# Delta stage: gate rows and inverse norms spread by row-repeating transfers through DRAM

## The reference, cut to what matters

```
g      = -exp(a_log) * softplus(a + dt_bias)          one number per head and token
G      = cumsum(g) within a chunk                      [16 heads, 256 tokens]
decay  = exp(G[i] - G[j]) for i >= j, else 0           128 x 128 for each head and chunk
A      = -beta * (k k^T) * decay;  T = (I - A)^-1      solved by blocks
o      = (q k^T * decay) v_new + (q * exp(G)) state    v_new and state from T, k, v
out    = (o * 1/sqrt(mean(o^2) + eps) * norm_w * silu(z)) @ w_out
```

## Time and profile before

| | us |
|---|---|
| median of 3 runs | 2250.34 |
| lowest, highest | 2249.08, 2255.46 |
| the profiled execution | 2247.1 |
| its span in the trace | 2245.3 |
| Delta stage in the trace, about | 1691 to 2044 |

### The profile page before, as it was taken

The page is one execution under the profiler, slowest core; times in us unless marked ns, Lnnn a source line. Parts: engine busy times, 40 slices in busy tenths (PEclk is TensorE's granted clock), DMA queues, the critical chain, the costliest instruction groups (busy, mean ns, idle before and its releaser), DMA issues.

```text
span 2245.3 us, 41478 instructions
## 1 busy us (share of the span) xinstructions
PE 2114.8 (94%) x15546; PEld 1969.2 (88%) x15546; DVE 1447.5 (64%) x2478; ACT 1114.0 (50%) x1802; POOL 48.6 (2%) x63
## 2 busy tenths in 40 slices
PE   7998999999998999999999999999997898999998
PEld 7977889999978889989998989989987787978997
DVE  4457677775457677776657666666667877457565
ACT  4454455555443455554445454454446566546443
POOL 1002000000002000000000000000000000000000
PEclk9899999999899999999999999999998998999999
DMA  8422355553222445546554555555554433335552
GB/s 248 150 95 85 121 193 185 195 194 132 89 99 83 146 160 196 194 143 214 181 193 164 174 179 186 179 172 187 183 169 122 127 109 114 112 123 183 187 186 95
DMA packets 118577, 350.80 MB, mean 156 GB/s; under 512 B 23505, under 2 KB 36121, under 8 KB 117953
## 3 DMA queue, kind: packets, MB, share of 16 engines
q1 hardware_dynamic: 115248, 336.27, 45.1%
q0 software_dynamic: 3216, 12.97, 2.1%
HBM read 341.85 MB, written 7.34 MB: 156 GB/s over the span
## 4 chain that ended last, share of the span: by engine, by line
PE 73%; DVE 13%; ACT 6%; issue 4%; DMA 2%; POOL 0%; DVEq 0%; ACTq 0%; SPq 0%; POOLq 0%
PE bank L2074 22%; PE bank L2076 21%; PE bank L2075 21%; DVE wlo L1392 5%; ACT whi L934 3%; PE bank L2500 1%; DMA raw<-panels 1%; PE bank L2223 1%; DVE arena L1582 1%; PE bank L2100 1%; DVE arena L1431 1%; PE bank L2283 1%; DVE x L1442 1%; DMA relay<-arena 0%; DMA arena<-relay 0%
## 5 line engine op out<-in xcount | busy, mean ns | idle before, releaser
L2074 PE MATMUL bank<-xhi,whi 128*128 128x256 f32 x3496 | 1007.2, 288 | 14.4 <-DVE xlo L1778 5.4
L2075 PE MATMUL bank<-xlo,whi 128*128 128x256 f32 x3496 | 993.7, 284 | 0.0
L2076 PE MATMUL bank<-xhi,wlo 128*128 128x256 f32 x3496 | 993.1, 284 | 0.0
L1392 DVE TENSOR_TENSOR wlo<-raw,whi 128x1024 fp32r<-128x1024 f32 x623 | 740.1, 1228 | 194.1 <-ACT whi L934 193.1
L2074 PEld LDWEIGHTS bank<-xhi,whi 128*128 128x128 f32 x3496 | 671.9, 192 | 34.0 <-issue 14.6
L2075 PEld LDWEIGHTS bank<-xlo,whi 128*128 128x128 f32 x3496 | 671.7, 192 | 6.1
L2076 PEld LDWEIGHTS bank<-xhi,wlo 128*128 128x128 f32 x3496 | 670.5, 192 | 0.0
L934 ACT ACTIVATE whi<-raw 128x1024 fp32r<-128x1024 f32 x623 | 623.7, 1046 | 57.4 <-DVE arena L1579 21.7
L2074 PE MATMUL bank<-whi,hhi 128*128 128x512 f32 x688 | 276.0, 401 | 12.6 <-DVE hlo L1533 6.3
L2076 PE MATMUL bank<-whi,hlo 128*128 128x512 f32 x688 | 273.9, 398 | 0.0
L2075 PE MATMUL bank<-wlo,hhi 128*128 128x512 f32 x688 | 273.7, 398 | 0.0
(11 more groups left out here) (361 smaller groups left out, 1784.3 us busy)
## 6 DMA issues: line engine op xcount, KB each, us to landing
raw<-panels SPq DMA_DIRECT2D x623, 512.0 KB, 4.3
arena<-w_in POOLq DMA_DIRECT2D x2, 2048.0 KB, 10.2
arena<-relay SPq DMA_DIRECT2D x8, 512.0 KB, 4.1
arena<-gains_in POOLq DMA_DIRECT2D x6, 512.0 KB, 3.9
relay<-arena POOLq DMA_DIRECT2D x4, 512.0 KB, 6.0
relay<-arena SPq DMA_DIRECT2D x4, 512.0 KB, 5.0
bias_table<-arena POOLq DMA_DIRECT2D x1, 1536.0 KB, 35.1
x<-x_in SPq DMA_DIRECT2D x1, 1024.0 KB, 5.0
```

Source lines behind the costliest of these rows:

```text
L1392: dve.tensor_tensor(wlo[slot][:], raw[slot][:], whi[slot][:].bitcast(F32), ALU.subtract) \
L2074: pe.matmul(dst, w_hi, a_hi, start=start, stop=False, skip_group_check=True)
L2075: pe.matmul(dst, w_hi, a_lo, start=False, stop=False, skip_group_check=True)
L2076: return pe.matmul(dst, w_lo, a_hi, start=False, stop=stop, skip_group_check=True)
```

## The change

`delta_rows` on PE goes. SP writes the 16 rows of `g_cum` to DRAM (`g_relay`) once, waits for that, and for each set reads four rows into `decay`, with a source whose partition step is zero, so that all 128 partitions get the same 4 KB. ACT computes `qg` from `decay` in one instruction and DVE then adds the mask to `decay` in place in one instruction. As both use one tile, DVE waits for ACT. The one-hot products of banks 6 and 7, and the waits that guarded these banks, go from PE.

The two products a block for the inverse norms go too. PE transposes `o_inv` in two parts (turn 41, and after `down` in block 2), ACT copies each, SP writes it to `o_relay`, waits, and reads it back row-repeated into four tiles that are free by then (`qmat[0]`, `tri_t[0]`, `wmat`, `tri`), 512 KB each. DVE takes the inverse norms from there.

```diff
+            def delta_rows_in(n):
+                if n == 0:
+                    sp.wait_ge(d["gates_ready"], 3)
+                    sp.dma_start(g_relay, g_cum[ROW_A:ROW_A + VH, :]).then_inc(d["g_out"], 16)
+                    sp.wait_ge(d["g_out"], 16)
+                else:
+                    sp.wait_ge(d["qmat"], KSET * n)
+                    sp.wait_ge(d["k_tail"], n)
+                sp.dma_start(decay.rearrange("p h c n -> p h (c n)"),
+                             bass.AP(g_relay.tensor, SET * n * S, [[0, P], [S, SET], [1, S]])).then_inc(d["g_rows"], 16)
+            def delta_o_rows(part):
+                cs = slice(0, 3 * SET * CHUNKS) if part == 0 else slice(3 * SET * CHUNKS, VH * CHUNKS)
+                sp.wait_ge(d["k_o_copied"], SETS + part + 1)
+                sp.dma_start(o_relay[cs, :], o_turned(part)).then_inc(d["g_out"], 16)
+                sp.wait_ge(d["g_out"], 16 * (part + 2))
+                sp.wait_ge(*reached("l64_sum", SETS - 1, "u"))
+                sp.wait_ge(d["o_sum"], 2 * (SETS - 1))
+                for g in (range(3) if part == 0 else (3,)):
+                    home = (qmat[0], tri_t[0], wmat, tri)[g]
+                    sp.dma_start(home.rearrange("p h c n -> p h (c n)"),
+                                 bass.AP(o_relay.tensor, SET * g * S, [[0, P], [S, SET], [1, S]])) \
+                        .then_inc(d["o_rows"], 16)
...
+                    if t == 8 * n - 1 + 2 * late(n):
+                        delta_rows_in(n)
...
+                if t == 8 * 2 + 25:
+                    delta_o_rows(0)
+            for p in range(loaded, first_panel[s] + PANELS[DELTA] + 2):
+                if p == first_panel[s] + PANELS[DELTA] - 8:
+                    delta_o_rows(1)
+                load(p)
...
-                for g in range(KSET):
-                    act.wait_ge(d["exponent"], KSET * n + g + 1)
-                    act.activation(qg[n % 3][:, 2 * g:2 * g + 2, :],
-                                   bank[6 + g][:].rearrange("p (h c i) -> p h c i", h=2, c=2)[:, :, 1, :],
-                                   ACT.Exp).then_inc(d["eg"], 1)
+                act.wait_ge(d["g_rows"], 16 * (n + 1))
+                act.activation(qg[n % 3], decay[:, :, 1, :], ACT.Exp).then_inc(d["eg"], 1)
+                act.wait_ge(d["exponent"], n + 1)
...
-                    dve.wait_ge(d["g_rows"], KSET * n + g + 1)
-                    dve.tensor_tensor(mats(decay)[:, 4 * g:4 * g + 4, :],
-                                      bank[6 + g][:].rearrange("p (m n) -> p m n", m=4),
-                                      masks[:, 2:3, :].to_broadcast([P, 4, P]), ALU.add).then_inc(d["exponent"], 1)
+                dve.wait_ge(d["g_rows"], 16 * (n + 1))
+                dve.wait_ge(d["eg"], n + 1)
+                dve.tensor_tensor(mats(decay), mats(decay), masks[:, 2:3, :].to_broadcast([P, MATS, P]), ALU.add) \
+                    .then_inc(d["exponent"], 1)
...
-                    dve.wait_ge(d["o_rows"], f + 1)
+                    dve.wait_ge(d["o_rows"], 16 * 3 if f < 3 * SET else 16 * 4)
                     dve.scalar_tensor_tensor(out=second[:, sl, :], in0=o_head(f), scalar=col(("out_norm", s)),
-                                             in1=bank[6 + sl][:, 0:S], op0=ALU.mult, op1=ALU.mult) \
+                                             in1=o_rows_of(f), op0=ALU.mult, op1=ALU.mult) \
...
-                        for c in range(CHUNKS):
-                            i = CHUNKS * f + c
-                            last = pe.matmul(bank[6 + f % 2][:, c * P:(c + 1) * P],
-                                             o_inv[:, i:i + 1].to_broadcast([P, P]), ident, start=True, stop=True)
-                        last.then_inc(d["o_rows"], 1)
                     if f:
                         down(s, f - 1, down_panel(s, f - 1), turn)
+                    if kind == DELTA and f == 2:
+                        delta_turn_o(1)
...
-            def delta_rows(s, n):
...
-                    pe.wait_ge(d["exponent"], KSET * n)
-                    pe.wait_ge(d["eg"], KSET * n)
...
+            def delta_turn_o(part):
+                cs = slice(0, 3 * SET * CHUNKS) if part == 0 else slice(3 * SET * CHUNKS, VH * CHUNKS)
+                pe.wait_ge(d["o_inv"], part + 1)
+                pe.wait_ge(*reached("l64", SETS - 1, "u"))
+                pe.transpose(bank[6 + part][0:cs.stop - cs.start, 0:P], o_inv[:, cs], ident) \
+                    .then_inc(d["k_o_turned"], 1)
```

More of the change, by code:

```diff
@@ L426, in relay_full, with o_turned, o_rows_of @@
             return bass.AP(relay.tensor, (2 * i + n % 2) * MATS * MAT_PITCH, [[P, P], [MAT_PITCH, MATS], [1, P]])
+        o_relay = nc.dram_tensor("o_relay", [VH * CHUNKS, P], F32, kind="Internal").ap()
+        g_relay = nc.dram_tensor("g_relay", [VH, S], F32, kind="Internal").ap()
+        def o_turned(part):
+            n = (3 * SET, SET)[part] * CHUNKS
+            return blk_a[0:n, part * P:(part + 1) * P]
+        def o_rows_of(f):
+            home = (qmat[0], tri_t[0], wmat, tri)[f // SET]
+            return home.rearrange("p h c n -> p h (c n)")[:, f % SET, :]
         def by_block(v):
@@ L531, in build @@
             "tile_read tap convolved activated squared gates_scaled gate_act gates_ready gate_turned gate_tok tok_exp "
-            "norm_sums norm_ms k_root v_turned v_copied g_rows exponent eg decay qg kk amat k_turned k_copied "
-            "k_tail qk qmat blocks_out blocks_in solved turned_blocks inverse_out tri_in tri_t_in cleared relay_zeroed "
+            "norm_sums norm_ms k_root v_turned v_copied g_rows exponent eg decay qg kk amat k_o_turned k_o_copied "
+            "k_tail qk qmat blocks_out blocks_in solved turned_blocks inverse_out tri_in tri_t_in cleared relay_zeroed g_out "
             "inverse_t_out "
@@ L1313, in delta_o_root, with delta_o_turned @@
                 act.activation(o_norm[:, 1, cs], o_norm[:, 0, cs], ACT.Sqrt).then_inc(d["o_root"], 1)
+            def delta_o_turned(part):
+                act.wait_ge(d["k_o_turned"], SETS + part + 1)
+                act.activation(o_turned(part), bank[6 + part][0:o_turned(part).shape[0], 0:P], ACT.Copy) \
+                    .then_inc(d["k_o_copied"], 1)
             def delta_step(s, n, o):
@@ L1359, in delta @@
                         delta_o_root(0)
+                    if t == 8 * 2 + 25:
+                        delta_o_turned(0)
                 delta_o_root(1)
@@ L1857, in delta_exponent @@
             def delta_exponent(n):
[L1859 to L1862, removed]
-                    dve.wait_ge(d["g_rows"], KSET * n + g + 1)
-                    dve.tensor_tensor(mats(decay)[:, 4 * g:4 * g + 4, :],
-                                      bank[6 + g][:].rearrange("p (m n) -> p m n", m=4),
-                                      masks[:, 2:3, :].to_broadcast([P, 4, P]), ALU.add).then_inc(d["exponent"], 1)
+                dve.wait_ge(d["g_rows"], 16 * (n + 1))
+                dve.wait_ge(d["eg"], n + 1)
+                dve.tensor_tensor(mats(decay), mats(decay), masks[:, 2:3, :].to_broadcast([P, MATS, P]), ALU.add) \
+                    .then_inc(d["exponent"], 1)
             def delta_qg(n):
-                dve.wait_ge(d["eg"], KSET * (n + 1))
+                dve.wait_ge(d["eg"], n + 1)
                 dve.wait_ge(d["activated"], 8 * n + 2 * KSET)
@@ L2147, in body @@
                             spread_rstd(s)
-                    if kind == DELTA:
-                        for c in range(CHUNKS):
-                            i = CHUNKS * f + c
-                            last = pe.matmul(bank[6 + f % 2][:, c * P:(c + 1) * P],
-                                             o_inv[:, i:i + 1].to_broadcast([P, P]), ident, start=True, stop=True)
-                        last.then_inc(d["o_rows"], 1)
                     if f:
                         down(s, f - 1, down_panel(s, f - 1), turn)
+                    if kind == DELTA and f == 2:
+                        delta_turn_o(1)
                 run_blocks(pe, s, body)
@@ L2474, in delta_turn_k @@
                     last = pe.transpose(bank[0][:, g * P:(g + 1) * P], keys(n)[:, g, 0:P], ident)
-                last.then_inc(d["k_turned"], 1)
+                last.then_inc(d["k_o_turned"], 1)
             def delta_qk(n):
@@ L2676, in delta @@
                         delta_step(s, n, t - 8 * n)
+                    if t == 8 * 2 + 25:
+                        delta_turn_o(0)
             pe.wait_ge(consts_ready, 4)
```

19 lines of the change are left out of this document (6 added, 13 removed).

## The result

The changed kernel takes 2256.27 us (median of 20 runs, 2251.55 to 2260.63), the kernel before 2249.54 beside it (20 runs, 2243.45 to 2256.4). The ratio is 1.0029, with a 95% interval of 1.002 to 1.0038: slower by about 6.5 us (the medians themselves differ by 6.7). The time lies in the predicted range, but the forecast was no change. The profiled execution of the changed kernel took 2251.55, the fastest of its 20, so its trace shows less than the median does: 2251.55 - 2247.1 = 4.4 us.

The account below looks back on a forecast made before the run. The prediction read the last-ending chain as 73% PE and 13% DVE, with PE often not setting the pace in the Delta stage. Its terms summed to -0.1 us, giving 2250.2 us as median, range 2243 to 2259.

Parts of the forecast that it names:

- The one in block 2 is hidden by what follows: Norm products: PE's added transpose in block 2 costs nothing, as the work after it hides it.
- forecast -1.9: Start of the blocks' loop: the third `second` no longer waits for rows, so the loop starts 1.9 us earlier.
- Set 0, +3.7: Set 0: DVE's addition, waiting for ACT's exp(G), ends 4.2 us later; less 0.53 us of idle time, 3.7 us lost.
- Set 1, +1.2: Set 1: the addition ends 3.9 us later, DVE's later waits absorb part, and 1.2 us is lost.
- by the sum above the level of each stretch stays as it is: PE's clock: the summed forecast assumes that fewer products on a waiting PE leave each stretch's clock level unchanged.
- third rival: PE's clock stays low longer, at `down` of block 1 and one stretch in the sets: +1.8 to +4 us, chance 0.08.
- Sets 2 and 3, -0.8 each: Sets 2 and 3: PE's merge products begin about 0.8 us sooner in each; bounds -1.9 and +2.0.
- The transpose of turn 41, +0.3: Turn 41: PE has one transpose more, costing 0.3 us, the length of the products it resembles.
- Blocks 12 to 15, -1.8: Blocks 12 to 15: PE sets the pace there, so four rows products of 0.44 us removed save 1.8 us.
- Transfers at nothing: Eight added row reads cost nothing, covered by PE's and ACT's work; without cover, 3.9 us more each.
- rival 4: A transfer is late: the norms' write and reads after turn 41 land late, a loss of 3 us, 2253; chance 0.03.
- Rival 2: DVE's wait for ACT is carried in every set, with no slack absorbing it: +8.2 us, 2258.5; chance 0.17.

Follow-up runs that it names:

- own_tile: The changed kernel with the row reads in a tile of their own, so DVE's addition does not wait for exp(G): 2253.77 us, ratio 1.0014.
- gates_only: The changed kernel with the inverse norms by PE products as before, so only the gate rows come by transfer: 2253.91 us, ratio 1.0026.
- own_copy_later_rows_kept: The changed kernel with a tile for the row reads, ACT's second copy in block 4, and all four sets' unread row products kept: 2247.94 us, ratio 0.9995.
- before_exp_first: The kernel before with only the order turned: DVE's mask addition waits for ACT's exp(G); the "order" column: 2254.74 us, ratio 1.0035.
- rows_kept_unread: The changed kernel with PE still making the four sets' row products, which nobody reads; the "rows" column: 2254.15 us, ratio 1.0035.
- norms_only: The changed kernel with the gate rows by PE products as before, so only the inverse norms come by transfer: 2250.93 us, ratio 1.0002.
- own_tile_rows_kept: The changed kernel with a tile of their own for the row reads and the unread row products kept on PE: 2249.65 us, ratio 1.0007.
- copy_later: The changed kernel with ACT's copy of the second transposed norms in block 4, not block 2: 2254.54 us, ratio 1.0018.

## Why the prediction was wrong, point by point

**Where the +4.4 of the trace lie against the -0.1 of the sum.** By the table: blocks 0 to 3 missed by 0.85 + 1.9 = 2.75, the blocks from 3 to the end by 1.8 - 0.73 = 1.07, the sets (turn 34) by 3.94 - 3.3 = 0.64, and turns 34 to 43 with the stretch to block 0 by 0.1: 4.5 in all. The last of these is small by luck: 1.6 us were lost there and 1.3 given back, both by the clock in the main, for which the sum had no term. The rest up to the 6.7 of the medians is how the traced execution of each kernel stands to its median: 4.7 below it after, 2.4 before.

**"The one in block 2 is hidden by what follows": wrong, the largest miss.** PE's transpose is nearly free, but ACT's copy of it waits 2.43 us behind `down` of block 1, and the rounding of the panel on which the loop turns stands behind it. The prediction priced the transpose on PE and not the copy, which the step adds to ACT's stream. With the copy in block 4 the forecast -1.9 comes out at -1.4 to -1.95. Shown by three pairs.

**Set 0, +3.7: right.** 3.30 after, 3.11 by order alone, nothing with a tile of its own. The 4 us waits, their releaser and their place were as predicted.

**Set 1, +1.2: right for the order, wrong in the whole.** Order alone cost 1.07 from turn 8 to 16; after lost 2.8 and peaked at +7.5 in turn 12. The difference is the clock. The step that failed is "by the sum above the level of each stretch stays as it is". The third rival had the mechanism, but looked for it first at `down` of block 1, and for one stretch of 2 us in the sets. It came in the sets, in set 1, and own_tile shows it alone: 4.3 us from turn 8 to 12, of which 1.4 is given back by turn 16. "PE's 1.92 us are worth nothing here" was too kind: without them the set lost. The set's 2.8 us are also past the 1.2 that the prediction gave as a sign of being wrong.

**Sets 2 and 3, -0.8 each: of the right kind, the size not settled.** From turn 16 to 34 after gave 2.1 and gates_only, whose sets are the same, 0.3; the forecast was 1.6. With the wait and the products both there the two sets cost 2.0 (order and rows in the table), so the products' removal gave 2.3 to 4.1 of the 3.8 that PE spent on them. These are single traces, and two of one step differ by 1.8, again with the clock: from turn 16 to 24 after takes 50.73 us at 1.00, gates_only 54.52 at 0.87; from there to turn 34 after takes 62.89 at 0.84, gates_only 60.99 at 0.89.

**The transpose of turn 41, +0.3: mis-sized.** From turn 41 to 42 after loses 0.11 us.

**Blocks 12 to 15, -1.8: right on PE, but only 0.7 of it reached the end.** PE's row products of blocks 12 and 15 before:

```profile
2018.11 0.60 PE L2152 MATMUL bank<-masks,arena 128*128 128x128 f32 x4
...
2036.36 0.61 PE L2152 MATMUL bank<-masks,arena 128*128 128x128 f32 x4
```

Those of blocks 13 and 14 start at 2024.19 and 2030.27: 6.08 or 6.09 us apart each time, and PE is not idle from 2015.27 to 2042.57. After, PE's up products start at 2019.22, 2024.86, 2030.49 and 2036.12, some 5.64 apart, as forecast. From the first of them to `down` of block 14 PE needs 19.75 us in place of 21.45, 1.7 less. But then it waits before `down` of block 15, and these last two `down` take 6.82 us in place of 5.84:

```profile
2042.75 0.47 PE L2124 MATMUL bank<-whi,hhi 128*128 128x512 f32 x1 [0.83 <-DVE hlo L1587]
```

The chain of the changed kernel, in order of time, for one of these blocks and the last:

```profile
2020.36 1.05 ACT whi L981
2021.43 2.36 DVE wlo L1446 x2
2023.79 0.35 DVE first L1529
2024.16 0.43 ACT act_out L1034
...
2024.71 0.43 DVE h L1585
...
2036.85 3.50 DVE wlo L1446 x3
```

It runs through ACT and DVE, with no PE in it until the last `down`. DVE's `second` of blocks 12, 13, 14 and 15 starts at 2020.09, 2025.23, 2030.92 and 2037.10 before, at 2024.04, 2029.18, 2034.33 and 2040.60 after: distances of 5.14, 5.69, 6.18 against 5.14, 5.15, 6.27. The estimate of 5.2 for DVE and ACT was right (5.14), save for the last block, which has three splits in a row (3.50 us) and which I had not counted. The step that failed is that PE still sets the pace once its products are gone: it does not in the last block, where `hlo` comes behind the three splits.

**Blocks 3 to 11 keep 3.56: right** (3.57). **Transfers at nothing: right.** All eight rows lay ready, and with PE's old work in place the sets stand where they stood before (own_copy_later_rows_kept); rival 4 didn't come.

**Rival 2, the wait carried, +8.2, was the nearest.** Its mechanism is shown, its size is not: by turn 34 after lost 3.9 us, the rival had 3.7 + 3.9 + 2.0 + 2.0 = 11.6, the forecast 3.3. Before_exp_first lost 6.2 there, and the forecast's terms without the two sets' 1.92 that it does not take away make 3.3 + 3.8 = 7.1. So the wait was priced about right, and the change is slower because what should pay it back did not come: 2.75 us in block 2, 1.07 in the last blocks, and the clock in set 1. Rival 3, the clock, had the right mechanism for the last of these.

**The clock after the sets: no term in the prediction.** The z reads of turns 34 to 38 keep their distances in every trace. The read of turn 39 then starts 1.5 us later in after, 2.9 in before_exp_first, own_tile and rows_kept_unread, and is on time in norms_only and own_copy_later_rows_kept. From the read of turn 38 to that of turn 39, before first, then after, then own_tile:

```profile
1935.10:1941.88 6.78, 5.91 (x105) 5.64 (x104) 2.72 (x7) 3.80 (x7) 0.00 (x0) 1.00 0.23 77
```

```profile
1937.83:1946.12 8.29, 7.42 (x104) 7.15 (x104) 2.72 (x6) 3.79 (x7) 0.00 (x0) 0.79 0.36 117
```

```profile
1937.90:1947.58 9.68, 8.81 (x104) 8.51 (x104) 2.72 (x6) 3.79 (x7) 0.00 (x0) 0.65 0.31 110
```

PE does the same work there, behind the same wait of 0.87 us for ACT, and the clock alone differs. In the thirteen traces the stretch takes 6.8 us at 1.00 (four), 8.3 at 0.79 (three) or 9.7 at 0.65 (six). Ahead of block 0 the clock works the other way round. PE's last sums of squares of set 3, before, then after:

```profile
1970.91 1.87 PE L2620 MATMUL bank<-ones,psq 128*128 128x1 f32 x8 [0.87 <-ACT psq L1306]
```

```profile
1975.27 1.05 PE L2642 MATMUL bank<-ones,psq 128*128 128x1 f32 x8 [0.87 <-ACT psq L1353]
```

So block 0 comes 1.3 us closer to turn 43 in after: 0.8 by the clock (0.97 from the last z read to block 0, against 0.83), and 0.44 because the first block waits for no rows, which norms_only has too.

**Left open.** What decides where the clock falls was not settled, and it is not the program alone. Up to block 2 own_tile_rows_kept and own_copy_later_rows_kept have the same instructions, and the first loses 1.5 us before turn 39, the second nothing. After and copy_later are alike up to there as well, and stand at 3.94 and 5.83 at turn 34.

## What to carry to other kernels

When a change lets two engines share one tile, look at who comes last to it: an order turned round costs the earlier engine the whole distance to the later one, and everything in its in-order stream, here 4 us a set. Price every instruction that a moved step issues on every engine, a copy of 0.27 us above all when it must wait on an engine with a long product ahead. Work taken from an engine that waits anyway gives nothing and can lower its clock; take it away where the engine sets the pace, and leave it where it doesn't. When the engine that sets the pace gets faster, ask which one sets it next, and in which block. And read steps of 1 to 2 us from several traces: two traces of the same instructions differed by 1.9 us here.

## What the runs showed of the hardware

- Four products (1.92 us) more or less ahead of a wait went with PE's level: clock 1.00 or 0.73 over the same 19 us, and 3.8 us of time at turn 12 (own_tile with and without them). Extra, unread products in one set are part of the fastest kernel of this study.
- About 100 matmul records of PE, the same each time, with a wait of 0.87 us for ACT in them, take 6.8 us at a granted clock of 1.00, 8.3 at 0.79 and 9.7 at 0.65 (turn 38 to 39 in thirteen traces). The same kernel instructions gave 1.00 in one trace and 0.79 in another.
- Over the runs of one kernel, the time goes down by about 2 us for each 0.001 of mean granted clock (1.6 to 2.6, a line through the runs of each kernel), and most of their spread goes with it (the farthest run lies 4 to 12 us from the median). Between kernels this does not hold: rows_kept_unread has a higher clock than after and its ratio is no lower.
- A row-repeating read of 4 KB to 128 partitions, 512 KB, lands in 4.5 to 5.0 us, against 4.0 for the gains in the same trace.
